# First expert unit's weights all fetched in the router stage, next unit's in the loop; tokens rounded first, rows turned before the mask

## The reference

```python
def moe_swiglu(u, router, w_gate, w_up, w_down):
    """Top-2-of-8 SwiGLU experts; all experts evaluated, weighted by the sparse renormalised gate."""
    logits = (u @ router).astype(jnp.float32)
    top_v, top_i = lax.top_k(logits, TOP_K)
    top_w = jax.nn.softmax(top_v, axis=-1)
    combine = jnp.sum(jax.nn.one_hot(top_i, N_EXPERTS, dtype=jnp.float32) * top_w[..., None], axis=-2)
    hidden = jax.nn.silu(jnp.einsum('bld,edf->blef', u, w_gate)) * jnp.einsum('bld,edf->blef', u, w_up)
    hidden = hidden * combine.astype(u.dtype)[..., None]
    return jnp.einsum('blef,efd->bld', hidden, w_down)
```

## Time and profile before

| | |
|---|---|
| median of 3 runs | 2137.04 us (2135.58 to 2139.24) |
| the profiled execution, its own time | 2134.37 us |
| its span, first to last instruction | 2132.6 us |
| mean granted clock of TensorE | 0.961 of full |
| PE busy | 1959.1 us (92%) |
| DVE, ACT busy | 1285.0 us, 1044.8 us |
| DMA queue q1, share of the 16 engines | 35.9% |
| router stage, first DMA issue to last matmul | 1435.31 to 1460.36 us of the span |
| expert stage, PE's first and last matmul | 1471.18 to 2095.93 us of the span |

### The profile page before, as it was taken

One profiled execution on the slowest core, in us unless ns is written; L12 is line 12 of the kernel. 1 busy time (PEld: TensorE's weight loads), 2 busy tenths in 40 slices (PEclk: granted clock), 3 DMA queues, 4 the chain that ended last, 5 costly groups with the idle time before them and its releaser, 6 DMA issues. The chain is left out here.

```text
span 2132.6 us, 33196 instructions
## 1 busy us (share of the span) xinstructions
PE 1959.1 (92%) x11838; PEld 1667.6 (78%) x11838; DVE 1285.0 (60%) x1934; ACT 1044.8 (49%) x1672; POOL 94.8 (4%) x62
## 2 busy tenths in 40 slices
PE   4998899897999999996998899887999999999993
PEld 2996555597999999996996555776888888888883
DVE  3725666564323233334816666545888888888886
ACT  4214344543211121225224344545888888888884
POOL 0320000000000000000310000002000000000001
PEclk9999999898999999997999999898999999999997
DMA  6205512202232222301205700119985381927464
GB/s 249 93 26 198 196 40 99 99 1 65 74 87 82 61 80 70 92 28 65 88 22 222 276 38 33 58 61 367 411 344 234 130 316 59 353 78 286 163 250 158
DMA packets 147368, 301.28 MB, mean 141 GB/s; under 512 B 17472, under 2 KB 85952, under 8 KB 144448
## 3 DMA queue, kind: packets, MB, share of 16 engines
q1 hardware_dynamic: 141552, 279.10, 35.9%
q0 software_dynamic: 2880, 10.49, 1.3%
q10 hardware_dynamic: 2832, 10.22, 1.2%
HBM read 368.16 MB, written 28.61 MB: 186 GB/s over the span
## 5 line engine op out<-in xcount | busy, mean ns | idle before, releaser
L2216 DVE TENSOR_TENSOR ex_wl<-ex_raw,ex_wh 128x1024 fp32r<-128x1024 f32 x351 | 419.2, 1220 | 25.9 <-ACT ex_wh L2094 14.3
L2094 ACT ACTIVATE ex_wh<-ex_raw 128x1024 fp32r<-128x1024 f32 x351 | 368.1, 1060 | 72.3 <-PE psum L2151 45.3
L2431 PE MATMUL psum<-norm_out,ex_w_hi 128*128 128x320 f32 x1408 | 264.4, 309 | 6.9 <-DVEq L2442 4.8
L2151 PE MATMUL psum<-ex_wh,ex_he_hi 128*128 128x512 f32 (+1 forms) x624 | 242.6, 389 | 11.0 <-issue 10.8
L2151 PE MATMUL psum<-ex_wl,ex_he_hi 128*128 128x512 f32 (+1 forms) x624 | 233.6, 374 | 0.0
L2151 PE MATMUL psum<-ex_wh,ex_he_lo 128*128 128x512 f32 (+1 forms) x624 | 233.0, 373 | 0.0
L2431 PEld LDWEIGHTS psum<-norm_out,ex_w_hi 128*128 128x128 f32 x1408 | 222.1, 188 | 7.6 <-DVE ex_sg L2441 5.2
L2345 ACT ACTIVATE ex_w_hi<-side 128x1024 fp32r<-128x1024 f32 (+1 forms) x60 | 68.4, 1144 | 225.0 <-PE psum L2431 189.4
L2431 PE MATMUL psum<-norm_out,ex_w_lo 128*128 128x320 f32 x704 | 160.3, 308 | 0.0
L2151 PEld LDWEIGHTS psum<-ex_wh,ex_he_hi 128*128 128x128 f32 x624 | 118.2, 189 | 33.2 <-issue 13.9
L2479 DVE TENSOR_TENSOR ex_hf<-psum,ex_sg 128x640 f32<-128x640 f32 x22 | 18.1, 825 | 199.5 <-PE psum L2431 199.5
(11 more groups left out here) (399 smaller groups left out, 3896.2 us busy)
## 6 DMA issues: line engine op xcount, KB each, us to landing
ex_raw<-moe_gate_up SPq DMA_DIRECT2D x236, 512.0 KB
ex_raw<-moe_w_down SPq DMA_DIRECT2D x143, 512.0 KB
x<-moe_gate_up SPq DMA_DIRECT2D x70, 512.0 KB
wmod_ssd<-w_mod SPq DMA_DIRECT2D x56, 512.0 KB, 5.9
wmod_at<-w_mod SPq DMA_DIRECT2D x24, 512.0 KB, 4.5
side<-ffn_w_gate SPq DMA_DIRECT2D x22, 512.0 KB, 3.9
side<-ffn_w_up SPq DMA_DIRECT2D x22, 512.0 KB, 5.0
side<-ffn_w_down SPq DMA_DIRECT2D x16, 704.0 KB, 4.9
```

The costliest lines, as they stand in the source:

```text
L2094: act.activation(wh[:, i % RING], raw_of(i), ACT.Copy).then_inc(*hi_done.up(1))
L2151: last = pe.matmul(p.psum[:, 2 + g % 2, 0:width], h[:, k], w[:, i % RING, cols], start=(k == 0 and m == 0), stop=(k == KD - 1 and m == 2))
L2216: dve.tensor_tensor(wl[:, i % RING], raw_of(i), wh[:, i % RING].bitcast(F32), ALU.subtract).then_inc(*lo_done.up(1))
L2431: last = pe.matmul(p.psum[:, 2 * PAIR[i] + half, 0:HT], w[:, SLOT[i], cols], m[:, k, half * HT:(half + 1) * HT], start=(k == 0 and n == 0) ...
```

## The change

Five edits, all in the router stage and the expert stage:

1. The router stage fetches all 33 pieces of the first unit (`EXPERT_PIECES`), not 20.
2. The loop of SyncE runs over the units but the first (`others`, a new word of the table, made by one more VectorE subtraction) and fetches in pass b the tokens and then the pieces of unit b + 1. The wait for the dispatch stands before the loop. The two rows of conditions are one now, and the waits for landed pieces in ScalarE's and TensorE's loops count one unit fewer, since the first unit's were counted in the router stage.
3. ScalarE rounds the first unit's tokens first, then reads the number of units, then waits for VectorE's zeros and stores them.
4. TensorE turns the row blocks 3 and 4 before it waits for the mask, not behind the counting matmuls.
5. The table is 17 words shorter and one longer.

The core of the diff:

```diff
-                for i in range(EARLY):
+                for i in range(EXPERT_PIECES):
                     sp.dma_start(expert_room(p, r, i), expert_piece(io, 0, i)).then_inc(
                         *p.sig(f"ex_raw_in{LANDINGS[LANDING_OF[i]][0]}_").up(16))
...
-                for b in range(1, 3):
+                for b in range(1, TB):
                     turn_rows(b)
 
                 pe.wait_ge(*mask_ready.at(1))
...
                 last.then_inc(*pos_ps.up())
-                for b in range(3, TB):
-                    turn_rows(b)
...
-                for n in range(2):
-                    dve.memset(fresh[:, n, 0:1], float(n))
-                    last = dve.tensor_tensor(fresh[:, n, 1:], eb[:, 1:], eb[:, 0:MAX_BLOCKS - 1], ALU.not_equal)
-                link(dve, last)
+                dve.memset(fresh[:, 0:1], 0.0)
+                dve.tensor_scalar(after[:], end[:, NE - 1:NE], 1.0, None, ALU.subtract)
+                link(dve, dve.tensor_tensor(fresh[:, 1:], eb[:, 1:], eb[:, 0:MAX_BLOCKS - 1], ALU.not_equal))
...
                 sp.wait_ge(*zeroed.at(len(credit) + 1))
                 n = n_blocks(sp)
-                with sp.Fori(0, MAX_BLOCKS) as b:
-                    with sp.If(b < n):
-                        e = sp.value_load(r["table"][0:1, bass.ds(b, 1)], min_val=0, max_val=NE - 1)
-                        later, fresh = (sp.value_load(r["table"][0:1, bass.ds(b + n * MAX_BLOCKS, 1)], min_val=0, max_val=1)
-                                        for n in (1, 2))
-                        for i in range(N):
-
-                            if i < SPLIT:
-                                sp.wait_ge(*lo_done.at(b * SPLIT + i + 1))
-                            else:
-                                sp.wait_ge(*piece_done.at(b * N + i + 1))
-                            sp.dma_start(raw_of(i), expert_piece(io, e, i),
-                                         cond=later if i < EARLY else fresh).then_inc(*raw_in[LANDING_OF[i]].up(16))
-                        sp.wait_ge(r["dispatched"], 16 * 2 * TB)
+                others = sp.value_load(r["table"][0:1, 2 * MAX_BLOCKS + 1:2 * MAX_BLOCKS + 2], min_val=0, max_val=MAX_BLOCKS - 1)
+                sp.wait_ge(r["dispatched"], 16 * 2 * TB)
+                with sp.Fori(0, MAX_BLOCKS - 1) as b:
+                    with sp.If(b < others):
                         sp.wait_ge(*x_turned.at(b + 2))
                         sp.dma_start(xg[:], slot_rows((b + 2) * SL)).then_inc(*x_in.up(16))
+                        e = sp.value_load(r["table"][0:1, bass.ds(b + 1, 1)], min_val=0, max_val=NE - 1)
+                        fresh = sp.value_load(r["table"][0:1, bass.ds(b + MAX_BLOCKS + 1, 1)], min_val=0, max_val=1)
+                        for i in range(N):
+
+                            if i < SPLIT:
+                                sp.wait_ge(*lo_done.at((b + 1) * SPLIT + i + 1))
+                            else:
+                                sp.wait_ge(*piece_done.at((b + 1) * N + i + 1))
+                            sp.dma_start(raw_of(i), expert_piece(io, e, i),
+                                         cond=fresh).then_inc(*raw_in[LANDING_OF[i]].up(16))
+                sp.wait_ge(*x_turned.at(n + 1))
+                sp.dma_start(xg[:], slot_rows((n + 1) * SL)).then_inc(*x_in.up(16))
...
+                take_tokens()
+                n = n_blocks(act)
                 act.wait_ge(*zeroed.at(len(credit) + 1))
                 act.dma_start(r["slots"][0:SL], ysb[:]).then_inc(*y_stored.up(16))
-                n = n_blocks(act)
-                act.wait_ge(*x_turned.at(2))
-                take_tokens()
...
-                            act.wait_ge(*raw_in[LANDING_OF[i]].at(16 * (hi - lo) * (b + 1)))
+                            act.wait_ge(*raw_in[LANDING_OF[i]].at(16 * (hi - lo) * b))
```

More of the change, by code:

```diff
@@ L1805, in stage_router @@
         before = sb("before", [P, MAX_BLOCKS, NE])
-        eb, fresh = sb("eb", [P, MAX_BLOCKS]), sb("fresh", [P, 2, MAX_BLOCKS])
+        eb, fresh, after = sb("eb", [P, MAX_BLOCKS]), sb("fresh", [P, MAX_BLOCKS]), sb("after", [P, 1])
         with nc.Block() as block:
@@ L1920, in _ @@
                 link(dve, dve.tensor_scalar(eb[:], eb[:], float(NE - 1), None, ALU.min))
-                for n in range(2):
-                    dve.memset(fresh[:, n, 0:1], float(n))
-                    last = dve.tensor_tensor(fresh[:, n, 1:], eb[:, 1:], eb[:, 0:MAX_BLOCKS - 1], ALU.not_equal)
-                link(dve, last)
+                dve.memset(fresh[:, 0:1], 0.0)
+                dve.tensor_scalar(after[:], end[:, NE - 1:NE], 1.0, None, ALU.subtract)
+                link(dve, dve.tensor_tensor(fresh[:, 1:], eb[:, 1:], eb[:, 0:MAX_BLOCKS - 1], ALU.not_equal))
                 dve.tensor_copy(r["table"][:, 0:MAX_BLOCKS], eb[0:1, :])
-                dve.tensor_copy(r["table"][:, MAX_BLOCKS:3 * MAX_BLOCKS], fresh[0:1].rearrange("p n b -> p (n b)"))
-                link(dve, dve.tensor_copy(r["table"][:, 3 * MAX_BLOCKS:3 * MAX_BLOCKS + 1], end[0:1, NE - 1:NE]))
+                dve.tensor_copy(r["table"][:, MAX_BLOCKS:2 * MAX_BLOCKS], fresh[0:1])
+                dve.tensor_copy(r["table"][:, 2 * MAX_BLOCKS:2 * MAX_BLOCKS + 1], end[0:1, NE - 1:NE])
+                link(dve, dve.tensor_copy(r["table"][:, 2 * MAX_BLOCKS + 1:2 * MAX_BLOCKS + 2], after[0:1]))
                 dve.wait_ge(*e2_done.at(1))
@@ L1965 @@
 LANDING_OF = [n for n, (lo, hi) in enumerate(LANDINGS) for _ in range(lo, hi)]
-EARLY = 20
 def expert_room(p, r, i):
@@ L2018, in n_blocks @@
         def n_blocks(eng):
-            return eng.value_load(r["table"][0:1, 3 * MAX_BLOCKS:3 * MAX_BLOCKS + 1], min_val=1, max_val=MAX_BLOCKS)
+            return eng.value_load(r["table"][0:1, 2 * MAX_BLOCKS:2 * MAX_BLOCKS + 1], min_val=1, max_val=MAX_BLOCKS)
         with nc.Block() as block:
@@ L2025, in _ @@
                 n = n_blocks(sp)
-                with sp.Fori(0, MAX_BLOCKS) as b:
-                    with sp.If(b < n):
-                        e = sp.value_load(r["table"][0:1, bass.ds(b, 1)], min_val=0, max_val=NE - 1)
-                        later, fresh = (sp.value_load(r["table"][0:1, bass.ds(b + n * MAX_BLOCKS, 1)], min_val=0, max_val=1)
-                                        for n in (1, 2))
+                others = sp.value_load(r["table"][0:1, 2 * MAX_BLOCKS + 1:2 * MAX_BLOCKS + 2], min_val=0, max_val=MAX_BLOCKS - 1)
+                sp.wait_ge(r["dispatched"], 16 * 2 * TB)
+                with sp.Fori(0, MAX_BLOCKS - 1) as b:
+                    with sp.If(b < others):
+                        sp.wait_ge(*x_turned.at(b + 2))
+                        sp.dma_start(xg[:], slot_rows((b + 2) * SL)).then_inc(*x_in.up(16))
+                        e = sp.value_load(r["table"][0:1, bass.ds(b + 1, 1)], min_val=0, max_val=NE - 1)
+                        fresh = sp.value_load(r["table"][0:1, bass.ds(b + MAX_BLOCKS + 1, 1)], min_val=0, max_val=1)
                         for i in range(N):
                             if i < SPLIT:
-                                sp.wait_ge(*lo_done.at(b * SPLIT + i + 1))
+                                sp.wait_ge(*lo_done.at((b + 1) * SPLIT + i + 1))
                             else:
-                                sp.wait_ge(*piece_done.at(b * N + i + 1))
+                                sp.wait_ge(*piece_done.at((b + 1) * N + i + 1))
                             sp.dma_start(raw_of(i), expert_piece(io, e, i),
-                                         cond=later if i < EARLY else fresh).then_inc(*raw_in[LANDING_OF[i]].up(16))
-                        sp.wait_ge(r["dispatched"], 16 * 2 * TB)
-                        sp.wait_ge(*x_turned.at(b + 2))
-                        sp.dma_start(xg[:], slot_rows((b + 2) * SL)).then_inc(*x_in.up(16))
+                                         cond=fresh).then_inc(*raw_in[LANDING_OF[i]].up(16))
+                sp.wait_ge(*x_turned.at(n + 1))
+                sp.dma_start(xg[:], slot_rows((n + 1) * SL)).then_inc(*x_in.up(16))
                 sp.wait_ge(*lo_done.at(n * SPLIT + TB))
@@ L2163, in _ @@
                                 lo, hi = LANDINGS[LANDING_OF[i]]
-                                pe.wait_ge(*raw_in[LANDING_OF[i]].at(16 * (hi - lo) * (b + 1)))
+                                pe.wait_ge(*raw_in[LANDING_OF[i]].at(16 * (hi - lo) * b))
                                 pe.wait_ge(*whole_done.at((b + 1) * WG + (f - SPLIT_F) // 2 + 1))
@@ L2650, in build @@
              "slot": p.sb("slot", [P, 2, TB], U32), "share": p.sb("share", [P, 2, TB]),
-             "table": p.sb("table", [1, 3 * MAX_BLOCKS + 2], I32), **slots}
+             "table": p.sb("table", [1, 2 * MAX_BLOCKS + 2], I32), **slots}
         with ExitStack() as lasting:
```

## The result

The changed kernel takes 2151.06 us (median of 4 runs, 2150.54 to 2151.55), the kernel before on the same chip 2136.31 us (2132.89 to 2139.24): a ratio of 1.0070, 95% interval 1.0052 to 1.0087, so it is slower, by 11 to 19 us. The whole difference is 0.7%, small but clear of the scatter of the runs. The two profiled executions are 17.1 us apart (spans of 2149.7 and 2132.6 us).

The account below looks back on a forecast made before the run. The loop is bound by TensorE, and the dispatch's landing sets the start of piece 8. Landing 15.8 plus clock 1.3 is 17.1 us slower: 2151.5 us profiled, 2154 us median (own range 2151 to 2158; 8 in 10, 2143 to 2158).

Parts of the forecast that it names:

- The dispatch sets piece 8, and the loop passes the shift on: Expert stage: the dispatch's landing sets TensorE's start of piece 8, 5.12 us later; any shift moves the end as much.
- The stage ends 5.7 us later since SyncE is held: Router stage: SyncE, held at about 10 outstanding transfers, ends it 5.7 us later; bounds nothing and 7 us.
- Even turns, landing 15.8 us later: DMA queues: q0 and q1 share the engines evenly, so the dispatch lands at 1496.1, 15.8 us later.
- my second estimate: DMA engines, from the whole: 13 more pieces, 6.82 MB, cost 16.1 us, so the dispatch lands at 1496.4.
- R1: Rival, DMA queues: the dispatch goes first, only the stage's start moves; +6.7 us, 2144 us; chance 0.15.
- R2: Rival, router stage: SyncE is not held, turns are even; +12.3 us and 1.3 of clock, 2150.6 us; chance 0.10.
- R3: Rival, router stage: not slower, all 33 issued within the stage, dispatch undisturbed; 1.1 us earlier, 2136 us; chance 0.08.
- The clock, 1.3 us: Expert stage: TensorE idles 13 us before piece 7, then runs 5.3 us at half clock, costing 1.3 us.
- Starting sooner, worth 0: Expert stage: first weights come 4.2 us earlier after the stage's start, worth 0 since the dispatch holds piece 7.
- Rows turned sooner, worth 1.1 us if TensorE ended the stage: Router stage: the gather starts up to 1.3 us earlier, worth 1.1 us, but 0 since SyncE ends the stage.
- The level, 2154 us: Whole kernel: 17.1 us on the profiled 2134.37 us gives 2151.5, median 2.7 us above it: 2154 us.

Follow-up runs that it names:

- e1: The changed kernel with 20 pieces fetched in the router stage and the other 13 behind SyncE's wait for the dispatch: 2134.46 us, ratio 1.0005.
- e3: The changed kernel with ScalarE's and VectorE's wait for the dispatch moved from before piece 7 to after piece 11: 2143.12 us, ratio 1.0044.
- e7: The kernel before, with only the wait for the dispatch moved from before piece 7 to after piece 11: 2132.96 us, ratio 1.0000.
- e2: e1 with the 13 later pieces issued as SyncE's first work in the expert stage, beside the dispatch: 2148.80 us, ratio 1.0073.
- e5: The changed kernel with the edits of e1 and e3 together: 2126.94 us, ratio 0.9971.
- e11: The kernel before, with only row blocks 3 and 4 turned before the mask: 2134.13 us, ratio 0.9999.
- e6: e5 with row block 4 turned behind the counting matmuls again, block 3 alone before the mask: 2125.74 us, ratio 0.9967.
- e9: e6 with 16 unused identity transposes added behind row block 4, filling TensorE's idle time before the gather: 2124.94 us, ratio 0.9955.
- e10: e9 with 40 more identity transposes at TensorE's start of the expert stage: 2124.13 us, ratio 0.9955.

## Why the prediction was right

*The dispatch sets piece 8, and the loop passes the shift on.* Right: e1 takes the loss away, e3 a good third of it by moving the wait alone, and units are 47.8 us apart in both kernels. Two readings of the kernel before were off. TensorE had not computed 8 pieces while the dispatch was under way, but had begun 29 matmuls, under 5 pieces, when it landed; and it came to piece 8 just 0.20 us early (at e7). That did not change the forecast of a later landing, but it hid that an earlier one could bring at most 0.2 us.

*The stage ends 5.7 us later since SyncE is held.* Right in effect: POOL's first dispatch came 33.2 us after the stage's start, not 26.1, so 7.1 us later, the far bound of mine. I took 10.2 outstanding pieces as the limit; at SyncE's end q1 had moved 12.51 MB of 17.3, 9.1 pieces less than issued, so SyncE's end came 1.2 us later after the start than I had it. And e2 shows that this term by itself decides nothing: without it the landing was only 1.1 us earlier.

*Even turns, landing 15.8 us later.* Measured 15.7, but not from the parts that I had. I had 5.7 us from the later stage and 10.1 from the longer way of the dispatch; they were 7.1 and 8.7 (from POOL's first issue to the landing 27.5 us, where it was 18.8). That the sum holds is no accident, since what is issued later finds fewer weights ahead of it, and my second estimate, from the whole of the bytes, does not ask where the stage ends. That it holds to 0.1 us is luck: landings with the same bytes ahead scatter by 1 us, q0's first packets came some 4 us after POOL's first issue where I took 3, and my two estimates gave 1496.2 and 1496.4, not the 1496.1 that I wrote. The 358 GB/s that I quoted beside them are not what this kernel gets (the engines moved 417 to 422 GB/s from 1477 to 1492), and the 19.0 us worked out by them are out. The shares of 35.3, 35.3 and 31.8%, and of 51.9 and 50.1%, are what the forecast was built on. The rule that the DMA engines take turns between the queues with work (the Trainium skill, DMA: Bandwidth & Descriptors, "Queues, rings and completion order") stands, by these rows, for a third pair too. R1, the dispatch served first, is out. So are R2 and R3, by SyncE's 17.01 us for the last eleven. The time alone would not have told R2 from the forecast: its 2150.6 us is nearer to the measured 2151.06 than my 2154.

*The clock, 1.3 us.* Piece 12 came 73.2 us after the stage's start and had come at 56.0: 17.2 us, of which 15.7 are the landing. The other 1.5 us are the clock, 0.2 more than I had. The idle time was 12.63 us, forecast as 13. The reason for the excess is, by the timelines, that piece 7 at half clock, with its transposes, took 3.36 us and so came out behind the rounding of piece 8 (which VectorE had ready by 1500.5, while TensorE began piece 8 at 1500.87), which I had as its cover.

*Starting sooner, worth 0.* Right for the changed kernel. In e1, where it stands alone, it is slightly below 0: TensorE started 4.8 us sooner, idled 4.94 us, and came to piece 12 0.8 us later than the kernel before, with a slow stretch of its clock in it. It is worth 6 us only with the wait moved (e5).

*Rows turned sooner, worth 1.1 us if TensorE ended the stage.* Wrong. It is worth nothing even then (e11), since the gather gives back in clock what it wins in start: the half clock that had fallen on the transposes now falls on it.

*The level, 2154 us.* The sum of 17.1 us is that of the profiled executions to the tenth, and to the tenth it is luck: the stage started 0.6 us sooner, piece 12 came 17.2 later after it, the loop added 0.8 and the part behind it took 0.3 less. I added it to a median of 2137.04, while the kernel before then ran at 2136.31, and the medians are 14.8 us apart, with an interval of 11 to 19.

## What to carry to other kernels

Before a transfer is moved to an earlier place, look for what is on the critical path in the same DMA engines between its old and its new place: here a prefetch that nobody waited for yet cost the dispatch 1.15 to 1.2 us for each piece, nearly the time in which the engines move one. And where two waits end together, take both away before judging either: here each alone gave nothing, and both together 6 us. The best versions measured keep the 20 early pieces, fetch the other 13 behind the dispatch, and wait for the dispatch at its first real conflict (e5, 0.9971; e6, 0.9967). Filling TensorE's idle time before the gather gave 0.9955 (e9 and e10), which their intervals do not tell from e6.

## What the runs showed of the hardware

- 80 matmuls of 128x128 took 9.20 us after 1.17 us of idle time, 9.17 after 0.38, 10.70 after 2.13 and 10.67 to 10.77 after 3.05 or 3.06 (nine runs). The granted clock in the first 3 us was 0.50 in the slow ones that were looked at (the changed kernel, e1, e6, e11) and 1.00 in the kernel before and e9. The idle time just ahead does not settle it: in e10 3 us of half clock came after 0.73 us of idle time, and in e9, whose program is the same up to there, none.
- How long the half clock lasts does not follow from the idle time ahead of it: 3.3 us after 6.21 us (e6), over 4.2 after the same 6.21 (e9, 0.50 from 1462.26 to 1466.50), 5.3 after 10.83, but 3.1 after 13.38 (the changed kernel at 1473.02, whose matmuls come 0.43 us apart up to 1476.1 and 0.23 after it), and over 5 after 12.63. What sets it stays open.
- SyncE's issue of a 512 KB transfer takes 0.3 to 0.7 us until some 10 of them, 5 MB, are outstanding, and then 1.1 us for most; in the changed kernel two of the last eleven took 3.8 and 3.0 us. Over these eleven that is 1.55 us each, where the engines need 1.28 for one at 408 GB/s.
